# Attention of a hybrid decoder step: eight blocks of exponentials turned in place of sixteen, the older keys' part by a triangle and a difference of values

## The reference

```python
WINDOW = 128; HEAD_DIM = 64; N_HEADS = 8; N_KV_HEADS = 2     # q heads 4n..4n+3 share kv head n
s = einsum(q, k) * HEAD_DIM ** -0.5
mask = (kpos >= 0) & (dq >= 0) & (dq < WINDOW)               # dq = qpos - kpos
s = where(mask, s, NEG_INF)
m = maximum(max(s, axis=-1), sink)
p = exp(s - m)
p = p / (sum(p, axis=-1) + exp(sink - m))
out = einsum(p, v)
```

## Time and profile before

| what | value |
|---|---|
| median of 3 runs | 826.24 us (826.08 to 828.62) |
| the profiled execution's own time | 825.75 us |
| its span in the trace | 822.9 us |
| PE busy | 747.6 us, 91% of the span |
| DVE busy | 396.3 us, 48% |
| ACT busy | 226.1 us, 27% |
| POOL busy | 219.2 us, 27% |

### The profile page before, as it was taken

One profiled execution on the slowest core, in us unless ns is written; L12 is line 12 of the kernel. 1 busy time (PEld: TensorE's weight loads), 2 busy tenths in 40 slices (PEclk: granted clock), 3 DMA queues, 4 the chain that ended last, 5 costly groups with the idle time before them and its releaser, 6 DMA issues.

```text
span 822.9 us, 11675 instructions
## 1 busy us (share of the span) xinstructions
PE 747.6 (91%) x4323; PEld 365.6 (44%) x4323; DVE 396.3 (48%) x1079; ACT 226.1 (27%) x549; POOL 219.2 (27%) x258
## 2 busy tenths in 40 slices
PE   6899999679999998999999915999999999999866
PEld 3666666436666664555555511323223232233322
DVE  0555655646284674567665563233333333222258
ACT  2756676511415235312111200111111111111123
POOL 1001100010111211122332257455544454431111
PEclk9999999778999998999999956999999999999978
DMA  9300120040101001577321766899999999999387
GB/s 326 142 27 26 41 103 1 5 157 1 40 18 58 0 1 51 211 268 298 127 78 52 272 256 200 334 409 421 410 416 412 417 414 415 417 414 406 139 335 283
DMA packets 32168, 172.78 MB, mean 210 GB/s; under 512 B 8915, under 2 KB 10123, under 8 KB 21850
## 3 DMA queue, kind: packets, MB, share of 16 engines
q1 hardware_dynamic: 21954, 153.30, 46.9%
q0 software_dynamic: 9632, 17.39, 5.8%
q10 hardware_dynamic: 528, 1.36, 0.5%
HBM read 154.90 MB, written 27.50 MB: 222 GB/s over the span
## 4 chain that ended last, share of the span: by engine, by line
PE 79%; DVE 8%; issue 5%; DMA 3%; ACT 3%; POOL 0%; DVEq 0%; SPq 0%; ACTq 0%; POOLq 0%
PE PS L1910 21%; PE PS L1926 10%; PE PS L1624 7%; PE PS L1761 6%; PE PS L1769 6%; PE PS L1745 4%; PE PS L1736 4%; PE PS L1625 3%; PE PS L1653 2%; PE PS L1725 2%; PE PS L1609 2%; DMA BIG<-ypair 2%; PE PS L1809 1%; PE PS L1640 1%; PE PS L1947 1%
## 5 line engine op out<-in xcount | busy, mean ns | idle before, releaser
L1910 PE MATMUL PS<-BIG,RD 128*32 128x512 f32 x1536 | 172.6, 602 | 22.5 <-DVE RD L1522 21.0
L1910 PEld LDWEIGHTS PS<-BIG,RD 128*32 128x32 f32 x1536 | 48.6, 111 | 128.9 <-issue 128.9
L759 POOL DMA_INDIRECT RD<-xtab,rot x96 | 96.8, 1008 | 30.3 <-issue 29.4
L1926 PE MATMUL PS<-BIG,RD 128*32 128x512 f32 x672 | 86.8, 592 | 0.0
L1500 DVE SCALAR_TENSOR_TENSOR RD<-RD,PS 128x256 f32<-128x256 f32 x25 | 10.5, 421 | 129.4 <-ACT RD L1001 129.4
L1624 PE MATMUL PS<-BIG 128*128 128x512 f32 x128 | 66.8, 604 | 3.8 <-DMA BIG<-in_wqkv 2.2
L1001 ACT ACTIVATE RD<-PS 128x256 f32<-128x256 f32 x25 | 9.6, 385 | 194.5 <-PE PS L1910 188.0
L783 POOL DMA_INDIRECT ypair<-RD,pids x25 | 25.9, 1034 | 131.1 <-DVE RD L1516 116.5
L1745 PE MATMUL PS<-BIG 128*128 128x344 f32 x192 | 58.8, 468 | 0.0
L1761 PE MATMUL PS<-BIG 128*128 128x512 f32 x128 | 58.2, 598 | 0.0
L1769 PE MATMUL PS<-BIG 128*128 128x512 f32 x128 | 57.7, 595 | 0.0
(11 more groups left out here) (293 smaller groups left out, 1051.8 us busy)
## 6 DMA issues: line engine op xcount, KB each, us to landing
BIG<-in_wexp SPq DMA_DIRECT2D x33, 2048.0 KB, 19.7
BIG<-in_wexp SPq DMA_DIRECT2D x29, 1024.0 KB, 23.6
BIG<-ypair SPq DMA_DIRECT2D x8, 1024.0 KB, 8.9
xin<-in_x SPq DMA_DIRECT2D x13, 512.0 KB, 4.0
BIG<-in_wxy SPq DMA_DIRECT2D x4, 1024.0 KB, 4.7
xin<-in_wexp SPq DMA_DIRECT2D x4, 1024.0 KB
BIG<-x2d SPq DMA_DIRECT2D x1, 4096.0 KB
out_y<-RD SPq DMA_DIRECT2D x8, 512.0 KB, 3.7
```

What stands on the lines that cost most here:

```text
L759: pool.indirect_dma_start(xg[:, p3, j * CHUNK_D:(j + 1) * CHUNK_D], None, xtab.rearrange("t (q e) -> (t q) e", q=NQ), bass.IndirectOffsetO ...
L1910: o = MM(PS[own, 2 + p2, :], xgT[:, p2, at:at + STRIP], wgu[expert(n, j) % NG][:, k * 512:(k + 1) * 512], start=(k == 0), stop=(k == KD - 1))
L1926: o = MM(PS[own, 5 + half, :], hT[:, p2, k, own], wdn[expert(n, j) % ND][:, at:at + 512], start=(k == 0), stop=(k == KF - 1))
```

## The change

`normalise` first adds the older half of each row's exponentials to the newer half (one instruction for four heads), and scales only the newer half. `turn_e` then turns 8 blocks, the sums. ACT copies the two banks of turned sums to PT[0] and PT[1]. DVE multiplies each by a triangle of ones and zeros (`lower`, a constant) into PT[2] and PT[3], which gives back the older keys' part; this takes the place of DVE's copy and of one of ACT's three copies. `values` adds sums x newer values and older part x (older values - newer values); the differences `vd` come from POOL. It has four matmuls of 512 columns, as before. The mask in the table of constants is kept once in place of twice, which makes the table 384 columns shorter net of the triangle. Semaphores count accordingly.

```diff
+            def v_step(b):
+                pool.wait_ge(v_ok, b + 1)
+                if b >= 2:
+                    pool.wait_ge(o_ps, b - 1)
+                nc.gpsimd.tensor_tensor(vd[:, b % 2, :], v_all[:, b, :], v_all[:, b + 1, :], ALU.subtract).then_inc(vd_ok, 1)
+
             for t in range(1, NT):
+                v_step(t - 1)
                 if t + 1 < NT:
                     rstd(t + 1)
                 sum_squares(t - 1)
...
                 softmax(b)
                 evict_qkv(t)
-                for q in (0, 2, 3):
-                    act.wait_ge(pt_ps, 2 * b + 1 + q // 2)
-                    A(PT[:, q, :], PS[:, q, :], ACT.Copy).then_inc(pta_ok, 1)
+                for lo in range(2):
+                    act.wait_ge(pt_ps, 2 * b + 1 + lo)
+                    A(PT[:, lo, :], PS[:, 2 * lo, :], ACT.Copy).then_inc(pta_ok, 1)
                 evict_q(t)
...
                 V.tensor_tensor(den[:, hs], rs[:, hs], es[:, hs], ALU.add).then_inc(dve_done, dq.up())
+                e2 = E[:, 2 * lo:2 * lo + 2, :].rearrange("q a (i two c) -> q (a i) two c", i=2, two=2)
+                V.tensor_tensor(e2[:, :, 1, :], e2[:, :, 0, :], e2[:, :, 1, :], ALU.add).then_inc(dve_done, dq.up())
                 dve.wait_ge(dve_done, dq.now())
                 V.reciprocal(rinv[:, hs], den[:, hs]).then_inc(dve_done, dq.up())
                 dve.wait_ge(dve_done, dq.now())
                 for h in range(4 * lo, 4 * lo + 4):
-                    e = E[:, h // 2, (h % 2) * 256:(h % 2 + 1) * 256]
+                    e = E[:, h // 2, (h % 2) * 256 + P:(h % 2 + 1) * 256]
                     V.tensor_scalar(e, e, rinv[:, h:h + 1], None, ALU.mult).then_inc(en_ok, 1)
 
-            def evict_pt(b, q):
-                dve.wait_ge(pt_ps, 2 * b + 1 + q // 2)
-                V.tensor_copy(PT[:, q, :], PS[:, q, :]).then_inc(ptd_ok, 1)
+            def mask_pt(b, lo):
+                dve.wait_ge(pta_ok, 2 * b + lo + 1)
+                V.tensor_tensor(PT[:, 2 + lo, :].rearrange("q (a c) -> q a c", a=4), PT[:, lo, :].rearrange("q (a c) -> q a c", a=4),
+                                lower.rearrange("q (o c) -> q o c", o=1).to_broadcast([P, 4, P]), ALU.mult).then_inc(ptd_ok, 1)
...
                     normalise(b, 1)
-                    evict_pt(b, 1)
+                    mask_pt(b, 0)
+                    mask_pt(b, 1)
                 dve.wait_ge(u_ok, t + 1)
...
                         pe.wait_ge(en_ok, 8 * b + h + 1)
-                        for kk in range(2):
-                            at = (h % 2) * 256 + kk * P
-                            o = TR(PS[:, 2 * lo + kk, k * P:(k + 1) * P], E[:, h // 2, at:at + P], ident)
+                        at = (h % 2) * 256 + P
+                        o = TR(PS[:, 2 * lo, k * P:(k + 1) * P], E[:, h // 2, at:at + P], ident)
                     o.then_inc(pt_ps, 1)
...
-                for kk in range(2):
-                    for lo in range(2):
-                        o = MM(PS[64 * lo:64 * lo + 64, 6, :], v_all[:, b + kk, 64 * lo:64 * lo + 64], PT[:, 2 * lo + kk, :],
-                               start=(kk == 0), stop=(kk == 1))
+                for lo in range(2):
+                    MM(PS[64 * lo:64 * lo + 64, 6, :], v_all[:, b + 1, 64 * lo:64 * lo + 64], PT[:, lo, :], start=True, stop=False)
+                for lo in range(2):
+                    pe.wait_ge(ptd_ok, 2 * b + lo + 1)
+                    o = MM(PS[64 * lo:64 * lo + 64, 6, :], vd[:, b % 2, 64 * lo:64 * lo + 64], PT[:, 2 + lo, :], start=False, stop=True)
                 o.then_inc(o_ps, 1)
```

More of the change, by code:

```diff
@@ L78 @@
 O_XS, O_HS, O_XL, O_HL, O_N = 0, 8, 16, 19, 20
-K_ID, K_UP, K_MASK, K_CS, K_THR, K_IE, K_IV, K_VALID = 0, 128, 256, 1280, 1856, 1864, 1896, 1920
-K_Q = 1920 + NT
+K_ID, K_UP, K_MASK, K_LOW, K_CS, K_THR, K_IE, K_IV, K_VALID = 0, 128, 256, 768, 896, 1472, 1480, 1512, 1536
+K_Q = 1536 + NT
 K_N = K_Q + 1
@@ L164, in build @@
         upper = cst[:, K_UP:K_UP + P]
+        lower = cst[:, K_LOW:K_LOW + P]
+        vd = sb("vd", [P, 2, KV])
         n_e, n_c, n_b = 2 * GUW + DNW, KD * D_MODEL, KD * NT * P
@@ L325, in build @@
         en_ok = sem("en_ok")
+        vd_ok = sem("vd_ok")
         kT_ok = sem("kT_ok")
@@ L379, in build @@
         xT2d_ok = ptd_ok
-        XT2D_OK = NPT
+        XT2D_OK = 2 * NPT
         r_ps = sem("r_ps")
@@ L1068, in maxima @@
             def maxima(b):
-                kind = K_MASK + (512 if b else 0)
+                kind = K_MASK + (256 if b else 0)
                 mask = cst[:, kind:kind + 256]
@@ L1637, in turn_e @@
                         pe.wait_ge(en_ok, 8 * b + h + 1)
-                        for kk in range(2):
-                            at = (h % 2) * 256 + kk * P
-                            o = TR(PS[:, 2 * lo + kk, k * P:(k + 1) * P], E[:, h // 2, at:at + P], ident)
+                        at = (h % 2) * 256 + P
+                        o = TR(PS[:, 2 * lo, k * P:(k + 1) * P], E[:, h // 2, at:at + P], ident)
                     o.then_inc(pt_ps, 1)
             def values(b):
-                pe.wait_ge(pta_ok, 3 * b + 3)
-                pe.wait_ge(ptd_ok, b + 1)
+                pe.wait_ge(pta_ok, 2 * b + 2)
+                pe.wait_ge(vd_ok, b + 1)
                 pe.wait_ge(xs_ok, 2 * min(b + 2, NT - 1) + 2)
@@ L1660, in turn_qk @@
                 if t >= 1:
-                    pe.wait_ge(pta_ok, 3 * t - 2)
+                    pe.wait_ge(pta_ok, 2 * t - 1)
                 for k in range(4):
@@ L2006, in constants @@
         m = np.where(ok, 0.0, MASKED)
-        c[:, K_MASK + 512 * kind:K_MASK + 512 * (kind + 1)] = np.concatenate([m, m], 1)
+        c[:, K_MASK + 256 * kind:K_MASK + 256 * (kind + 1)] = m
+    c[:, K_LOW:K_LOW + P] = np.tril(np.ones((P, P)), -1)
     inv = 10000.0 ** (-2.0 * np.arange(32) / HEAD_DIM)
```

## The result

| | before | with the change |
|---|---|---|
| median of the runs on one chip, us | 827.43 (826.08 to 829.25, 4 runs) | 836.37 (834.39 to 841.42, 4 runs) |
| profiled execution: time, span, us | 825.75, 822.9 | 836.07, 834.3 |
| one period of the attention loop, us | 17.43 | 18.83 |

The ratio is 1.0126 with a 95% interval of [1.0087, 1.0164]: 1.3% slower, which is 10.4 us of 827.43, where 11.2 were predicted. The two medians of four runs lie 8.9 us apart and the two profiled executions 10.3.

A forecast was written before the change was run, and what follows sets the result against it. The prediction took the attention loop to be bound by PE, with DVE's rotation almost at the edge. Steps 1 to 6 (8.3), step 7 (1.43) and step 8 (1.46) made 11.2 us on 826.24: 837.5 predicted, range 834.6 to 843.

The forecast's parts named there:

- The edge: DVE's rotation ends within 0.1 us of when PE would wait to turn q; any delay lengthens every period as much.
- The period: One attention-loop period, 17.43 us before, becomes 18.8, with q turned and done 1.38 us later.
- Steps 1 to 7: Attention loop: 1.38 us in each of steps 1 to 6, 8.3 together, and the whole 1.43 in step 7.
- PE's saving: Turning of exponentials: eight fewer transposes save 0.87 us a period, only about 0.2 usable because of v's copy.
- the rival in which PE's saving shows: Triangle hidden in the loop, PE gains 0.2 us in six steps, about 0.5 in step 8: 824.5 us; chance 0.04.
- The addition and POOL: Normalisation's 0.60 us addition stays hidden with 0.3 us cover; POOL's 0.46 us difference costs nothing.
- step 8: Last attention step, a bare chain with PE at half clock: rotation starts at 162.17 against 160.71, 1.46 us later.
- The sum: Attention loop total: 8.3 for steps 1 to 6, 1.43 for step 7, 1.46 for step 8, making 11.2 us.
- step 7: Attention step where PE already waited 1.54 us for the rotation, so the whole 1.43 us delay counts.
- The clock's rival: PE's clock falls in the loop's new waits, 2 to 3.5 us lost each time: 840 to 848; chance 0.14.
- nothing takes the loss back behind the loop: Later stages and their transfers start when the attention stage ends, so the whole 11.2 us remains.

The follow-up runs named there:

- fill_step7: Changed kernel plus three spare 512-column matmuls on PE ahead of the turning of q in step 7 alone: 834.8 us, ratio 1.0107.
- no_products: Changed kernel without the two triangle products, values reading the unmasked sums, so the older part is wrong: 825.52 us, ratio 0.9979.
- rot_first: Changed kernel with DVE's two triangle products moved behind the rotation: 825.25 us, ratio 0.9993.
- one_behind: Changed kernel with the first product ahead of the rotation and the second behind it: 829.08 us in one execution.
- third_product: Changed kernel with a third 512-element DVE product ahead of the rotation, written to an unread part of E: 849.06 us, ratio 1.027.
- pool_products: Changed kernel with both triangle products on POOL in place of DVE: 838.52 us in one execution.
- rot_first_fill: rot_first plus spare matmuls: one in step 7, four and two in step 8, three ahead of the diagonal's matmuls: 817.74 us, ratio 0.9893.
- rot_first_fill2: rot_first_fill with five in place of four spare matmuls in step 8 and one more between its turned halves: 830.69 us, ratio 0.9883.
- second_addition: rot_first plus a second 512-element addition in each half of the normalisation: 835.05 us in one execution; kernel before 840.49 on that chip.

## Why the prediction was right, and where it was off

**The edge.** The prediction said that the rotation ends within 0.1 us of the moment at which PE would wait, so that any delay of it lengthens the period. This held. With 0, 1, 2 and 3 products ahead of the rotation the period is 17.25, 18.23, 18.83 and 19.44: each further product costs 0.60 to 0.61, the predicted start-to-start distance. The first makes the rotation 1.36 us later, since it waits for ACT's copy, and the period 0.98 longer.

**The period.** Predicted 18.8 and +1.38; measured 18.83 and +1.40. The rotation was to start 1.43 later; 1.44 was measured. Steps 1 to 7 together: 9.7 predicted, 9.85 measured.

**PE's saving.** Eight transposes were to take 0.87 us, and 0.2 of the saving to be usable, because of v's copy. They start at 113.41 and PE then waits 0.42 for that copy; with the products out of the way the period falls by 0.19. So the rival in which PE's saving shows needed the products off the edge, and even then gives 0.9993 as a ratio, which cannot be told from no change.

**The addition and POOL.** Nothing waits for either in the changed kernel. A second addition would no longer be hidden.

**The step that was mis-sized is step 8.** The sum had +1.46 for it, with the clock low where it was low before. Measured: +4.2. The prediction looked for a fall of the clock in waits of some 1.5 us, and counted for step 7 only the 1.43 us by which its rotation is late. It did not add up what PE's wait there becomes: 1.54 us before, 1.52 by which the step is longer, and 0.32 that PE's own work is shorter, together the 3.38 of the row. The prediction's own rows had a fall in a wait of 4.01 us, and compared only 1.5 us with it. The clock fell in the wait of 3.38 us too. That is 2.5 us of the 4.2, which fill_step7 took away again; the remaining 1.67 are near the predicted 1.46.

**The clock's rival came true in part.** It had one fall at 2 to 3.5 us and a time of 840 or more. One fall came, in step 7's long wait and in none of the six full periods, and it cost 2.5 us. That the six waits of 1.37 us passed is what this trace shows and no rule: no_products lost its clock behind a wait of 1.43.

**Luck in the total.** The prediction said that nothing takes the loss back behind the loop. At the last turning of q the loss was 14.06 us, 2.9 more than predicted. Behind it 2.7 came back: 0.7 between the diagonal and the recurrent branch's first matmul (9.66 us before, 8.98 after), 1.3 up to the experts' first (322.24 and 320.90), 0.7 behind it. The first 0.7 is the clock: it fell earlier in the kernel before (155.6 to 176.1 us in one piece) than here (155.6 to 162.4, 169.3 to 182.9, 186.3 to 189.7), and the first two records of the diagonal's matmuls take 1.39 us in place of 2.07. The other 2.0 cannot be put down to the change. From the recurrent branch's first matmul to the end of the span the trace before has 643.8 us and the one after 641.8, but rot_first, one_behind, third_product, no_products, pool_products and fill_step7, whose instructions there are the same, have 644.8, 639.9, 642.8, 645.0, 643.2 and 641.3. One more microsecond went outside the span: the profiled execution's own time is 2.85 us longer than its span before, and 1.77 after, and no run shows why. So 14.06 - 2.7 - 1.1 makes the 10.3 between the two profiled executions. That this lies near the 11.2 of the sum is luck: a term that was 2.75 us too small met a return behind the loop of which most is within the variation of the traces. What was predicted rightly is steps 1 to 7, to 0.15 us.

## What to carry to other kernels

Before an instruction goes into an engine's queue, count what stands behind it: two products that take 1.29 us together cost nothing behind the rotation and 1.58 us a period ahead of it (17.25 and 18.83), since the first also carried a wait for another engine. Work taken from the busiest engine pays only up to the next edge; look for it (here the copy of v, for which PE waits 0.42 us) before counting the saving. And where an edit makes a wait of TensorE longer, add up the whole wait that results and ask whether the clock survives it. If it does not, spare matmuls into a free bank are a cheap test and may be a gain of their own.

## What the runs showed of the hardware that was not expected

POOL's product with two SBUF inputs takes 1.5 to 1.9 us for 512 elements, against 0.69 on DVE. Two of DVE's two-input instructions that started while it ran took 1.44 and 1.54 us for 0.49 and 0.48 and ended some 0.35 us behind POOL's; one that had started just ahead of it kept its time.

The length of PE's wait alone did not decide whether the clock fell. Behind waits of 1.97 us it fell in four of six cases in one kernel, behind a wait of 1.43 us in no_products and not behind the same wait in rot_first, behind waits of 0.93 and 0.98 us in rot_first_fill, and never behind the changed kernel's six waits of 1.37 us. Behind 1.97 us a fall cost 1.66 us.

The kernel before had medians of 826.68 to 827.43 on three occasions and 840.49 on a fourth, the one of rot_first_fill2 and second_addition. Whether that is the chip or the occasion was not tested. The ratios of two nearly equal kernels on two of these occasions agreed (0.9893 and 0.9883), so a kernel is compared with the kernel before on the same chip.
